# First feed-forward of a two-block transformer kernel: three more weight units with both parts of the activation side by side, and the copies and splits around them put in another order

## The reference

```python
h2 = rms_norm(x, norm_ffn_pre[l])
ff = jnp.einsum('bsf,fd->bsd',
                jax.nn.silu(jnp.einsum('bsd,df->bsf', h2, w_gate[l]))
                * jnp.einsum('bsd,df->bsf', h2, w_up[l]), w_down[l])
x = x + rms_norm(ff, norm_ffn_post[l])
```

## Time and profile before

| | |
|---|---|
| median of 3 runs | 804.32 us (804.22 to 804.37) |
| the profiled execution | 805.98 us, of which the profile's span is 804.2 us |
| instructions | 13648 |
| PE busy | 797.6 us, 99% of the span |
| DVE, ACT, POOL busy | 571.0, 465.2 and 109.4 us |
| HBM traffic | 177 GB/s over the span |

### The profile page before, as it was taken

How to read it: one execution, slowest core, us unless ns; L and a number is a source line. 1 busy time by engine, 2 the same in 40 slices (tenths; PEclk the granted TensorE clock), 3 DMA queues, 4 the chain that set the end, 5 groups by cost and what they waited for, 6 DMA issues and landing times.

```text
span 804.2 us, 13648 instructions
## 1 busy us (share of the span) xinstructions
PE 797.6 (99%) x5836; PEld 700.6 (87%) x5836; DVE 571.0 (71%) x713; ACT 465.2 (58%) x614; POOL 109.4 (14%) x82
## 2 busy tenths in 40 slices
PE   8999999999999999999999999999999999999998
PEld 7999988888888898888888889988899888888886
DVE  5877896796576587666676688688978865656653
ACT  6679784665534575454454575387787644444442
POOL 0101691662100000000000010111610100000000
PEclk9999999999999999999999999999999999999999
DMA  8744444453554555555555555456423555555541
GB/s 307 284 171 172 159 158 158 143 172 112 204 176 151 218 184 180 209 174 192 205 170 200 198 170 206 168 211 162 137 89 110 199 180 187 209 175 192 210 156 53
DMA packets 37820, 143.03 MB, mean 178 GB/s; under 512 B 9426, under 2 KB 11490, under 8 KB 24320
## 3 DMA queue, kind: packets, MB, share of 16 engines
q1 hardware_dynamic: 36576, 138.69, 49.7%
q0 software_dynamic: 1040, 3.43, 1.3%
q10 hardware_dynamic: 144, 0.04, 0.0%
HBM read 141.08 MB, written 1.06 MB: 177 GB/s over the span
## 4 chain that ended last, share of the span: by engine, by line
PE 96%; ACT 2%; DMA 2%; DVE 1%; issue 0%; POOL 0%; SPq 0%
PE ps L2392 8%; PE ps L2385 7%; PE ps L2032 6%; PE ps L2284 6%; PE ps L2285 6%; PE ps L2286 6%; PE ps L1964 6%; PE ps L2038 6%; PE ps L2035 6%; PE ps L1965 6%; PE ps L1966 6%; PE ps L2390 4%; PE ps L2387 4%; DMA raw<-w 2%; PE ps L2140 1%; PE ps L2300 1%
## 5 line engine op out<-in xcount | busy, mean ns | idle before, releaser
L1182 DVE TENSOR_TENSOR wlo<-raw,whi 128x2048 fp32r<-128x2048 f32 (+2 forms) x128 | 289.4, 2263 | 76.3 <-ACT whi L626 74.9
L626 ACT ACTIVATE whi<-raw 128x2048 fp32r<-128x2048 f32 (+2 forms) x128 | 241.3, 1888 | 105.6 <-DMA raw<-w 105.6
L1964 PE MATMUL ps<-xx,whi 128*128 128x256 f32 x396 | 114.1, 288 | 0.0
L1965 PE MATMUL ps<-xx,whi 128*128 128x256 f32 x396 | 112.0, 283 | 0.0
L1966 PE MATMUL ps<-xx,wlo 128*128 128x256 f32 x396 | 112.0, 283 | 0.0
L2284 PE MATMUL ps<-whi,xx 128*128 128x512 f32 x216 | 84.1, 389 | 0.0
L2285 PE MATMUL ps<-whi,xx 128*128 128x512 f32 x216 | 84.0, 389 | 0.0
L2286 PE MATMUL ps<-wlo,xx 128*128 128x512 f32 x216 | 84.0, 389 | 0.0
L2032 PE MATMUL ps<-whi,xx 128*128 128x512 f32 x208 | 83.0, 399 | 0.0
L2038 PE MATMUL ps<-wlo,xx 128*128 128x512 f32 x208 | 81.1, 390 | 0.0
L2035 PE MATMUL ps<-whi,xx 128*128 128x512 f32 x208 | 81.0, 390 | 0.0
(11 more groups left out here) (324 smaller groups left out, 1367.6 us busy)
## 6 DMA issues: line engine op xcount, KB each, us to landing
raw<-w SPq DMA_DIRECT2D x105, 1024.0 KB, 4.8
raw<-w SPq DMA_DIRECT2D x42, 512.0 KB, 5.0
raw<-w SPq DMA_DIRECT2D x8, 256.0 KB, 6.3
x<-xT SPq DMA_DIRECT2D x4, 256.0 KB, 5.7
work<-bias_scratch POOLq DMA_DIRECT2D x1, 1024.0 KB, 7.8
raw<-w SPq DMA_DIRECT2D x4, 192.0 KB, 3.3
out<-x SPq DMA_DIRECT2D x3, 256.0 KB, 2.5
raw<-w SPq DMA_DIRECT2D x3, 240.0 KB, 3.3
```

Of the source, the lines that this page charges most:

```text
L626: A(hi, full, ACT.Copy).then_inc(sem("hi_ready"), 1)
L1182: V.tensor_tensor(lo, full, hi.bitcast(F32), ALU.subtract)\
L1964: mm(out, hi, xh[:, tile, :], start=start, stop=False, skip_group_check=skip)
L1965: mm(out, hi, xl[:, tile, :], start=False, stop=False, skip_group_check=skip)
```

## The change

`WIDE1` now begins with pair 1, and unit 44 (up of pair 0) is wide as well. So units 44, 45 and 46 go the wide way: 44 into banks 0 and 2, 45 into banks 3 and 4, 46 into banks 1 and 7 (`ENTRY_BANKS`). `first_parts` stays for the unit at the start of the kernel, `pair_tiles`, `gate_scaled` with a pair number and `hidden` go. ScalarE copies the low columns of six more tiles; it brings in the silu table with an activation of one column ahead of the copy into `bcs`; and the copies of unit 45 stand on either side of `silu_pair(0)`. VectorE takes the low part of pair 0's product (`hidden_lo(0, ...)`) between the additions and the scaling of gate 1, and puts the split of unit 49 behind the product of pair 1.

```diff
-WIDE1 = range(2, PAIRS1)
+WIDE1 = range(1, PAIRS1)
+ENTRY_BANKS = ((0, 2), (3, 4), (1, 7))
...
-    units = []
+    units = [(U_F1 + 1, ENTRY_BANKS[0])]
     for j in WIDE1:
-        units += [(U_F1 + 3 * j - 1, GATE_BANKS), (U_F1 + 3 * j, UP_BANKS)]
+        gate, up = ENTRY_BANKS[1:3] if j == 1 else (GATE_BANKS, UP_BANKS)
+        units += [(U_F1 + 3 * j - 1, gate), (U_F1 + 3 * j, up)]
...
             split_hi(U_F1 + RING)
+            low_copy(U_F1 + 1, 0, lows[1])
+            low_copy(U_F1 + 1, 1, lows[1])
             split_hi(U_F1 + 1 + RING)
+            A(warm[:, :], half_s[:, 0:1], ACT.Silu)
             bc_copy("n3")
+            low_copy(U_F1 + 2, 0, lows[0])
             silu_pair(0)
+            low_copy(U_F1 + 2, 1, lows[0])
             hidden_hi(0, "hid", 0, 0)
...
                 count(low_added(u, 0, two(silu), lows[0]))
                 link(low_added(u, 1, two(silu), lows[0]))
+                if j == 1:
+                    hidden_lo(0, 0, "hid", 0)
                 V.tensor_tensor(two(silu), two(silu), factors_by_tile(2), ALU.mult).then_inc(sem("gate_r"), 1)
...
             norm_factors("n3", 1)
+            up_added(U_F1 + 1, 0)
+            up_added(U_F1 + 1, 1)
             split_lo(U_F1 + RING)
             dve.wait_ge(sem("norm_bcs"), before("bcs", "n3") + 1)
-            gate_scaled(0, U_F1, U_F1 % RING)
+            gate_scaled(U_F1, U_F1 % RING)
             split_lo(U_F1 + 1 + RING)
-            hidden(0, 0, U_F1 + 1, (U_F1 + 1) % RING)
-            hidden_lo(0, 0, "hid", 0)
+            silu_scaled(0)
+            hidden_wide(0, 0)
...
             first_unit(U_F1, 8, "n3")
-            first_parts(U_F1 + 1, 8)
+            pe.wait_ge(sem("hi_ready"), U_F1 + 2)
+            used(wide_tiles(U_F1 + 1, 8, low=lambda: arrived(U_F1 + 1)))
             norm_stats("n3", sq3)
...
-                if j in WIDE1:
+                if first:
+                    pe.wait_ge(sem("ple_copy"), PLE_EARLY // 2)
+                else:
                     pe.wait_ge(sem("gate_r"), j)
                     pe.wait_ge(sem("hid_y"), j)
-                    used(wide_tiles(u, 8))
-                else:
-                    used(pair_tiles(u, 8, between=lambda: norm_bc("n3")))
+                used(wide_tiles(u, 8, between=(lambda: norm_bc("n3")) if first else None))
                 pe.wait_ge(sem("lo_ready"), u + 2)
-                if j in WIDE1:
-                    used(wide_tiles(u + 1, 8))
-                else:
+                if first:
                     pe.wait_ge(sem("gate_r"), 1)
-                    used(pair_tiles(u + 1, 8))
+                used(wide_tiles(u + 1, 8, between=factors_read if first else None))
                 pe.wait_ge(sem("lo_ready"), u + 3)
                 pe.wait_ge(sem("hid_lo"), j)
                 if first:
-                    pe.wait_ge(sem("ple_copy"), PLE_EARLY // 2)
+                    pe.wait_ge(sem("gate_r"), 2)
```

More of the change, by code:

```diff
@@ L881, in _ @@
                 u = U_F1 + 3 * j - 1
-                wide = j in WIDE1
-                if wide:
+                if j > 1:
                     low_copy(u, 0, lows[0])
                 split_hi(u + RING)
-                if wide:
+                if j > 1:
                     low_copy(u, 1, lows[0])
-                    low_copy(u + 1, 0, lows[1])
+                low_copy(u + 1, 0, lows[1])
                 silu_pair(j)
@@ L891, in _ @@
                     split_hi(u + 1 + RING)
-                if wide:
-                    low_copy(u + 1, 1, lows[1])
+                low_copy(u + 1, 1, lows[1])
                 hidden_hi(j, "hid", 2 * (j % 2), j % 2)
@@ L1509, in _, with gate_scaled @@
             ahead(U_PLE)
-            def gate_scaled(j, u, bank):
+            def gate_scaled(u, bank):
                 dve.wait_ge(sem("unit_used"), u + 1)
-                if not isinstance(j, int) or j >= 1:
-                    dve.wait_ge(sem("gated"), j)
                 V.tensor_tensor(two(silu), two(ps[bank][:, :]), factors_by_tile(2), ALU.mult).then_inc(sem("gate_r"), 1)
[L1519 to L1529, removed]
             def low_added(u, m, out, low):
@@ L1541, in gate_wide, with silu_scaled, up_added @@
                 link(low_added(u, 1, two(silu), lows[0]))
+                if j == 1:
+                    hidden_lo(0, 0, "hid", 0)
                 V.tensor_tensor(two(silu), two(silu), factors_by_tile(2), ALU.mult).then_inc(sem("gate_r"), 1)
-            def up_wide(j, u, m):
-                if m == 0:
-                    dve.wait_ge(sem("silu"), j + 1)
+            def silu_scaled(j):
+                dve.wait_ge(sem("silu"), j + 1)
+                if j:
                     dve.wait_ge(sem("hid_y"), j)
-                    V.tensor_tensor(two(gated), two(silu), factors_by_tile(2), ALU.mult).then_inc(sem("gated"), 1)
+                V.tensor_tensor(two(gated), two(silu), factors_by_tile(2), ALU.mult).then_inc(sem("gated"), 1)
+            def up_added(u, m):
                 count(low_added(u, m, lows[1], lows[1]))
@@ L1555, in hidden_wide @@
                 dve.wait_ge(sem("dve_chain"), chained[0])
-                dve.wait_ge(sem("hid_lo"), j)
+                if j:
+                    dve.wait_ge(sem("hid_lo"), j)
                 V.tensor_tensor(hid[slot_h], two(gated), lows[1], ALU.mult).then_inc(sem("hid_y"), 1)
@@ L2363, in _, with wide_tiles @@
             used(ple_part(range(4, PLE_EARLY)))
-            def pair_tiles(u, base, between=None, bank=None):
-                bank = u % RING if bank is None else bank
-                for m in range(2):
-                    if between and m:
-                        between()
-                    for k in range(8):
-                        last = mm3(ps[bank][:, m * T:(m + 1) * T], u % SLOTS, (8 * m + k) * P, base + k, k == 0, k == 7)
-                return last
-            def wide_tiles(u, base, between=None):
+            def wide_tiles(u, base, between=None, low=None):
                 for m in range(2):
@@ L2385, in wide_tiles @@
                             mm(o[:, :], whi[:, u % SLOTS, w(k)], xx[:, base + k, :, :], start=k == 0, stop=False)
+                        if low:
+                            low()
                         for k in range(8):
@@ L2397, in _, with factors_read @@
             first_unit(U_F1, 8, "n3")
-            first_parts(U_F1 + 1, 8)
+            pe.wait_ge(sem("hi_ready"), U_F1 + 2)
+            used(wide_tiles(U_F1 + 1, 8, low=lambda: arrived(U_F1 + 1)))
             norm_stats("n3", sq3)
+            def factors_read():
+                pe.wait_ge(sem("norm_bcs"), before("bcs", "n3") + 1)
             def ffn1_step(j, u):
```

21 lines of the change are left out of this document (7 added, 14 removed).

## The result

| | kernel before | changed kernel |
|---|---|---|
| median | 804.41 us (804.22 to 805.31, 6 runs) | 809.63 us (806.21 to 811.09, 6 runs) |
| profiled execution | 805.98 us, span 804.2 | 808.98 us, span 807.2 |
| instructions | 13648 | 13566 |

The ratio is 1.0056, with a 95% interval of 1.0047 to 1.0066. The changed kernel is slower by more than 0.2%, a case to which I had given 2%; the forecast of 803.7 us and the range up to 804.6 are missed.

What follows compares the result with a forecast made beforehand. TensorE, busy 797.6 of 804.2 us, was taken as the bound. Three wide units at -0.195 us each, waits priced at nothing, gave -0.585 us: median 804.32 to 803.74, forecast 803.7, range 803.3 to 804.6 us.

Steps and rivals of the forecast that it cites:

- TensorE's saving: Units 44 to 46: wide instead of narrow matmuls save 0.195 us a unit, 0.585 us for three.
- Slacks: Units 44 to 49: partners finish before TensorE needs them, thinnest 0.27 us at unit 45 and 0.4 at unit 47.
- Rival 2: ScalarE's table load ahead of the copy into `bcs` costs twice, unit 46 waits 0.4 us: 804.1 to 804.6, chance 12%.
- Rival 3: VectorE's queue to `gate_r` 2 becomes the bound, TensorE waits 1.0 us at down unit 47: 804.7 us, chance 7%.
- Rivals 4 and 5: Units 44 to 46: saving only 0.12 us, 804.2, chance 4%; or more than the sum, 803.4, chance 7%.
- behind the place of the change nothing idles that could swallow it: After unit 44 TensorE works without pause, so the saved 0.585 us reaches the end unless a new wait takes it.

Runs made afterwards that it cites:

- experiment 9: Both kernels with 16, then 20, one-column fp32 matmuls added at the start: changed 804.5 and 804.55 us, before 806.65 and 805.32 us.
- changed + 192: Changed kernel with 48 one-column matmuls (192 instructions) added at the start: 808.78 us, ratio 1.0059 to the kernel before.

## Why the prediction was wrong

**TensorE's saving: right, mis-sized by 0.07.** Forecast 0.195 us a unit and 0.585 in all, measured 0.51 in the rows and 0.50 to 0.51 in the account of each changed kernel without added groups (seven traces); controls show 0.00. By the timeline unit 46 takes 303.27 - 297.71 = 5.56 us, as forecast; units 44 and 45, each up to the start of the next, take 5.92 us. For 44 that was 6.08 before, 0.16 less and not 0.195, and the same is left for 45: the missing 0.07 lies in the two units that have sums or broadcasts put between their matmuls. By the fixed 2.5 ns for each matmul of the Trainium skill (TensorE: Matmul & The Clock Gate, section "Wait — 56ns, not 53.3ns?"), which I weighed against the row, the estimate was 0.12; measured is 0.51, so the row was the better guide.

**Slacks: right.** Unit 46 starts at 297.71 (forecast 297.9, with the start 0.33 earlier here), the down unit at 303.27 (forecast 303.5). The thinnest slack, 0.27 us at unit 45, held; gate 1 was scaled at 302.24, ahead of my 302.7 to 303.1. No engine of the feed-forward is waited for.

**Rival 2** (the table load costs twice): 1.30 us between the load's start and the next activation, no wait behind it. **Rival 3** (VectorE's way to `gate_r` 2): 1.0 us of slack left. **Rivals 4 and 5**: the saving lies 0.07 below the forecast, far from 0.12, and no more than forecast was saved. None of them is what happened, and the slower side had its mechanism at the wrong place.

**The step that failed** is "behind the place of the change nothing idles that could swallow it", and with it "time saved in its row of matmuls reaches the end unless a new wait takes it". I looked for new waits among the partners that the diff names and among semaphores. Removing 96 instructions also moves every later instruction by 96 against the blocks in which TensorE's stream arrives, and at 519 us a burst of 320 instructions in 1.5 us runs through blocks faster than they come. In the kernel before, the end lay 179 instructions in and the burst passed with no standstill: with an end at 19 the standstill is 2.37 us, and 1.51 more go to the clock that falls after it. The sum is -0.51 + 3.88 = +3.4 us, against the +3.0 between the two profiled executions, whose starts differ by -0.33 to -0.43.

The Trainium skill, Runtime: NRT & Kernel Launch, section "Instruction fetch mechanics", describes refills in blocks of 256 instructions and calls the cost of crossing one "mostly hidden". The blocks of 256 agree with every row above; that it is hidden holds for wide matmuls, and not for this burst, where the trace has 2.1 to 2.7 us.

**What stays open.** The medians lie 5.2 us apart and the trace accounts for 3.4. The 3.4 belong to one execution of each kernel; the changed kernel's own runs spread over 4.9 us (granted clock 0.995 to 0.999), and I have one trace of them. How long the lower clock lasts, and late transfers as in experiment 9, may make up the rest; that is not shown. The path from block end to packet was read from times, not taken apart.

## What to carry to other kernels

On a kernel that is bound by one engine, a change of the number of its instructions moves all later block ends: find the places with about 256 instructions or more in under 4 us (bursts of tiny matmuls), and count where the ends fall before and after. To judge a small change then, time it at two or three shifts beside controls with the same shift, and read a running account of landmarks rather than the median. Cut such a burst in two: the halves cost 0.40 us here and took the standstill away with the block ends unmoved; other positions of the ends were not run with the burst in two. No version beats the kernel before by more than these runs can tell: the burst in two is at 0.9993 (0.9983 to 1.0003), the changed kernel shifted by 64 at 1.0006 (0.9995 to 1.0016).

## What the runs showed of the hardware that I had not expected

- The instruction stream of TensorE can stop it: in three kernels behind instructions 8385, 8641 and 8641, for 2.37, 2.72 and 2.10 us. The packet started 1.2 to 1.6 us after a block end was passed (518.58, 524.10, 518.51), and TensorE went on some 2.4 us later (519.79 to 522.23, 525.66 to 528.10, 519.96 to 522.32), so 3.7 to 4.0 us from end to use. Where TensorE took 3.4 us over the same way (changed + 192) no wait is listed. Wide matmuls with their loads need about 29 us for 256 instructions (128 at 0.225), far from the danger.
- Behind a standstill of 2.37 us and of 2.72 us the granted clock was at 0.50 for over 3 us, which added 1.5 and 1.8 us; the second time the fall began only 1.4 us after TensorE had gone on. Behind a wait of 2.27 us for VectorE it fell as well; behind the standstill of 2.10 us it stayed at 1.00.
- A change from wide to tiny matmuls and back costs some 0.33 us.
- Tiny matmuls ahead of the first products (48 and 80 calls) went with a clock of 0.66 and 0.53 in the stretches from 9 us on, and made the start 3 to 6 us longer; 16 and 20 calls did not.
- A table load of 1.28 us between two activations costs its own length and 0.02 us.
